# Norm factors by a power on GpSimd in place of a square root on ScalarE and a reciprocal on VectorE

## The reference

```python
def _rms_norm(x, gain):
    xf = x.astype(jnp.float32)
    y = xf * lax.rsqrt(jnp.mean(xf * xf, axis=-1, keepdims=True) + EPS)
    return (y * gain.astype(jnp.float32)).astype(x.dtype)
...
    for l in range(DEPTH):                       # first block
        xn = _rms_norm(x, attn_norm[l])
        h = xn @ w_in[l]                         # split into nine parts
        c_q = _rms_norm(h_cq, mla_q_norm[l])     # and c_kv; q and k of 16 heads are normed too
...
        o_b = (_rms_norm(o_b, diff_out_gain[l]) * (1.0 - lambda_init)).astype(x.dtype)
...
        x = x + mix @ w_o[l]
        xn = _rms_norm(x, ffn_norm[l])
        gate, up = jnp.split(xn @ w_gate_up[l], 2, axis=-1)
        x = x + (jax.nn.silu(gate) * up) @ w_down[l]
...
        x = x + rmsnorm(merged @ w_out[l], norm_mix_post[l])     # second block
        h = rmsnorm(x, norm_mem_pre[l])
        mem_n = rmsnorm(mem, norm_memkv[l])
        x = x + rmsnorm(memory_cross_attention(h, mem_n, w_mq[l], w_mkv[l], w_mo[l]), norm_mem_post[l])
        h = rmsnorm(x, norm_ffn_pre[l])
```

## Time and profile before

| | us |
|---|---|
| median of three runs | 1974.97 (1973.1 to 1977.52) |
| the profiled execution, its own time | 1970.69 |
| span of its trace | 1968.9 |
| TensorE busy in it | 1823.7 |
| VectorE busy | 1125.8 |
| ScalarE busy | 907.2 |
| GpSimd busy | 226.9 |

### The profile page before, as it was taken

One profiled execution on the slowest core, in us unless ns is written; L12 is line 12 of the kernel. 1 busy time (PEld: TensorE's weight loads), 2 busy tenths in 40 slices (PEclk: granted clock), 3 DMA queues, 4 the chain that ended last, 5 costly groups with the idle time before them and its releaser, 6 DMA issues.

```text
span 1968.9 us, 35037 instructions
## 1 busy us (share of the span) xinstructions
PE 1823.7 (93%) x13640; PEld 1709.3 (87%) x13640; DVE 1125.8 (57%) x1564; ACT 907.2 (46%) x1297; POOL 226.9 (12%) x104
## 2 busy tenths in 40 slices
PE   5999899998998899999999996999799999869997
PEld 5976799998965799998999885999789998859997
DVE  3553465542564365536564775775365647757763
ACT  5444544435354453434354455545243544555442
POOL 3520100004520200000000301000100003010000
PEclk9996999998987999999999998999899999989999
DMA  6420255444320345535534531655254445316551
GB/s 239 133 67 11 70 169 183 158 166 163 116 65 11 102 161 191 184 141 175 178 129 144 175 131 62 207 185 190 93 175 167 139 135 177 134 65 203 185 192 49
DMA packets 52447, 276.60 MB, mean 140 GB/s; under 512 B 5936, under 2 KB 6320, under 8 KB 51888
## 3 DMA queue, kind: packets, MB, share of 16 engines
q1 hardware_dynamic: 51984, 272.14, 41.2%
q10 hardware_dynamic: 288, 2.10, 0.3%
HBM read 273.16 MB, written 1.05 MB: 139 GB/s over the span
## 4 chain that ended last, share of the span: by engine, by line
PE 86%; DVE 7%; issue 4%; ACT 3%; DMA 0%; DVEq 0%; POOL 0%; ACTq 0%; SPq 0%; POOLq 0%
PE bank L704 22%; PE bank L706 21%; PE bank L707 21%; PE scores L883 2%; PE bank L663 2%; PE bank L666 1%; PE heads L908 1%; PE turned L896 1%; PE scores L716 1%; PE scores L713 1%; PE scores L715 1%; PE turned L908 1%; PE bank L1172 1%; PE bank L823 1%; PE bank L672 1%
## 5 line engine op out<-in xcount | busy, mean ns | idle before, releaser
L704 PE MATMUL bank<-x_hi,weights_lo 128*128 128x256 f32 (+1 forms) x2512 | 720.8, 287 | 5.6 <-DVE x_lo L1862 4.7
L707 PE MATMUL bank<-x_hi,weights_hi 128*128 128x256 f32 (+1 forms) x2512 | 713.1, 284 | 0.0
L706 PE MATMUL bank<-x_lo,weights_hi 128*128 128x256 f32 (+1 forms) x2512 | 713.1, 284 | 0.0
L617 DVE TENSOR_TENSOR weights_lo<-raw,weights_hi 128x1536 fp32r<-128x1536 f32 (+2 forms) x302 | 516.7, 1735 | 288.2 <-ACT weights_hi L606 287.7
L606 ACT ACTIVATE weights_hi<-raw 128x1536 fp32r<-128x1536 f32 (+3 forms) x352 | 498.2, 1439 | 118.3 <-PE bank L707 79.9
L704 PEld LDWEIGHTS bank<-x_hi,weights_lo 128*128 128x128 f32 (+1 forms) x2512 | 481.5, 192 | 13.0 <-issue 6.3
L706 PEld LDWEIGHTS bank<-x_lo,weights_hi 128*128 128x128 f32 (+1 forms) x2512 | 481.6, 192 | 2.5 <-issue 1.9
L707 PEld LDWEIGHTS bank<-x_hi,weights_hi 128*128 128x128 f32 (+1 forms) x2512 | 481.6, 192 | 0.0
L630 POOL TENSOR_TENSOR weights_lo<-raw,weights_hi 128x1536 fp32r<-128x1536 f32 (+4 forms) x50 | 165.0, 3308 | 676.1 <-ACT weights_hi L606 676.0
L706 PE MATMUL bank<-hidden_lo,weights_hi 128*128 128x256 f32 x704 | 199.6, 284 | 0.0
L707 PE MATMUL bank<-hidden_hi,weights_hi 128*128 128x256 f32 x704 | 199.6, 284 | 0.0
(11 more groups left out here) (294 smaller groups left out, 2641.1 us busy)
## 6 DMA issues: line engine op xcount, KB each, us to landing
raw<-in_w_b SPq DMA_DIRECT2D x194, 768.0 KB, 4.5
raw<-in_w_a SPq DMA_DIRECT2D x122, 768.0 KB, 4.5
raw<-in_w_a SPq DMA_DIRECT2D x14, 512.0 KB, 3.5
raw<-in_w_b SPq DMA_DIRECT2D x10, 512.0 KB, 3.9
mem<-in_mem ACTq DMA_DIRECT2D x2, 1024.0 KB, 4.9
raw<-in_w_a SPq DMA_DIRECT2D x2, 752.0 KB, 4.2
raw<-in_w_b SPq DMA_DIRECT2D x2, 752.0 KB, 4.3
raw<-in_w_b SPq DMA_DIRECT2D x2, 720.0 KB, 5.3
```

Of the source, the lines that this page charges most:

```text
L617: nc.vector.tensor_tensor(wlo[c % SPLIT][:, 0:n], raw[c % RAW][:, 0:n], whi[c % SPLIT][:, 0:n].bitcast(F32), ALU.subtract).then_inc(*s.mar ...
L704: ins = nc.tensor.matmul(dst, wl, xh, start=start, stop=False, skip_group_check=skip)
L706: nc.tensor.matmul(dst, wh, xl, start=False, stop=False, skip_group_check=skip)
L707: ins = nc.tensor.matmul(dst, wh, xh, start=False, stop=stop, skip_group_check=skip)
```

## The change

The columns of ones in the sum matmuls become columns of 1/n, so that the sum is the mean already. VectorE adds epsilon while it reads the bank (`tensor_scalar`, into `norm_mean`, `head_mean` or `dif_mean`). GpSimd raises that to the power -0.5 with a `tensor_tensor` whose second operand is a constant tile of -0.5. ScalarE takes no roots; its dummy roots are gone. What waits for a factor is as before.

```diff
-    put("half_sums", (half[:, None] == np.arange(2)[None, :]).astype(np.float32))
+    put("half_means", (half[:, None] == np.arange(2)[None, :]).astype(np.float32) / np.float32(DIF_D))
+    put("minus_half", np.full((P, 16), -0.5, np.float32))
+    for n in (DM, MLA_QR, MLA_KVR, DIF_V, MLA_QK):
+        put(f"mean_{n}", np.full((P, 2), 1.0, np.float32) / np.float32(n))
...
-        def load_root_table(tag):
-
-            n = 52 + ("o", "mem", "mo", "down", "latent").index(tag)
-            nc.scalar.activation(ROW[:, n:n + 1], eps_col, ACT.Sqrt)
-
         def scalar_norm(pl, act, l, tag, src, ready):
             scalar_squares(pl, act, l, tag, src, ready)
-            scalar_root(pl, act, l, tag)
+            if tag == "n1":
+                split_hi(pl, act, l, 1)
...
-        def scalar_root(pl, act, l, tag):
-            s = pl.s
-            if tag == "n1":
-                split_hi(pl, act, l, 0)
-            act.wait_ge(*s.at(l, "filled", f"{tag}_sum"))
-            nc.scalar.activation(NROOT[:, 0:4], pl.bank(f"{tag}_sum")[:, 0:4], ACT.Sqrt, scale=1.0 / DM, bias=eps_col)\
-              .then_inc(*s.mark("norm_root", tag))
-            if tag == "n1":
-                split_hi(pl, act, l, 1)
...
         def vector_norm_sum(pl, dve, l, tag):
             s = pl.s
-            dve.wait_ge(*s.at(l, "norm_root", tag))
-            nc.vector.reciprocal(NFACT[:, 0:4], NROOT[:, 0:4]).then_inc(*s.mark("norm_factor", tag))
+            dve.wait_ge(*s.at(l, "filled", f"{tag}_sum"))
+            nc.vector.tensor_scalar(NMEAN[:, 0:4], pl.bank(f"{tag}_sum")[:, 0:4], EPS, None, ALU.add).then_inc(*s.mark("norm_mean", tag))
...
-                ins = nc.tensor.matmul(ps[:, 2 * m:2 * m + 2], squares_of(tag)[:, 0, m * P:(m + 1) * P], ones[:, 0:2], start=True, stop=True)
+                ins = nc.tensor.matmul(ps[:, 2 * m:2 * m + 2], squares_of(tag)[:, 0, m * P:(m + 1) * P], const(f"mean_{DM}"), start=True, stop=True)
...
-                    dve.wait_ge(*s.at(l, "qk_root", name))
-                    nc.vector.reciprocal(HFACT[:, i, :], HROOT[:, i, :]).then_inc(*s.mark("qk_factor", name))
+                    dve.wait_ge(*s.at(l, "filled", f"{name}_sum"))
+                    nc.vector.tensor_scalar(HMEAN[:, i, :], pl.bank(f"{name}_sum")[:, 0:8], EPS, None, ALU.add)\
+                      .then_inc(*s.mark("qk_mean", name))
...
                     y = Y[:, 2 * i:2 * i + 2, :]
+                    dve.wait_ge(*s.at(l, "y_scaled", f"{POST[tag]}{i}"))
                     nc.vector.tensor_tensor(y, y, factor, ALU.mult).then_inc(*s.mark("norm_n", (tag, i)))
...
+        def inverse_root(pool, pl, l, out, mean, done, key):
+            s = pl.s
+            pool.wait_ge(*s.at(l, *mean[1]))
+            n = out.shape[-1]
+            nc.gpsimd.tensor_tensor(out, mean[0], const("minus_half")[:, 0:n], ALU.pow).then_inc(*s.mark(done, key))
+
         def pool_layer(pl, pool, l, order):
             pl.s.writing = "pool"
             pl.pool_next = 0
             for kind, name in order:
                 if kind == "squares" or kind == "norm" and ("squares", name) not in order:
                     pool_norm(pl, pool, l, name)
+                if kind == "norm":
+                    inverse_root(pool, pl, l, NFACT[:, 0:4], (NMEAN[:, 0:4], ("norm_mean", name)), "norm_factor", name)
+                elif kind == "latent":
+                    inverse_root(pool, pl, l, NFACT[:, 0:8], (NMEAN[:, 0:8], ("norm_mean", "latent")), "norm_factor", "latent")
+                elif kind == "turn" and pl.number == 0:
+                    i = qk_place(name)[0]
+                    inverse_root(pool, pl, l, HFACT[:, i, :], (HMEAN[:, i, :], ("qk_mean", name)), "qk_factor", name)
+                elif kind == "dif_sum":
+                    inverse_root(pool, pl, l, OFACT[:, :], (OMEAN[:, :], ("dif_mean", 0)), "dif_factor", 0)
                 elif kind == "job":
                     pool_lo(pl, pool, l, pl.last_chunk(name) + 2)
...
         @block.gpsimd
         def _(pool):
+            pool.wait_ge(loaded["const"], 16)
```

More of the change, by code:

```diff
@@ L461, in const @@
             return CM[:, a:b]
[L463 removed]
+        ident, ones, half_means = const("ident"), const("ones"), const("half_means")
         KB = (const_at["turn_dil"][0], consts.shape[1])
@@ L1030, in transformer @@
             order_a += [("map", i)] + between.get(i, [])
-        order_a += [("root_table", "o")] + [("job", f"o{i}") for i in range(4)]
+        order_a += [("job", f"o{i}") for i in range(4)]
         order_a += [("norm", "n2"), ("spread", "n2")]
@@ L1034, in transformer @@
             order_a += [("job", f"gate{i}"), ("job", f"up{i}")]
-        order_a += [("root_table", "down")] + [("job", f"down{i}") for i in range(4)]
+        order_a += [("job", f"down{i}") for i in range(4)]
         def free_a(name):
@@ L1076, in transformer @@
             elif kind == "dif_sum":
-                uses_a.append(("dif_sum", ("dif_root", 0)))
+                uses_a.append(("dif_sum", ("dif_mean", 0)))
             elif kind == "dif_spread":
@@ L1162, in tensor_a @@
                     _, at, fam, rows = next(q for q in qk_jobs if q[0] == name)
-                    heads_of = ones[0:rows, 0:2] if fam == "mla" else half_sums
+                    heads_of = const(f"mean_{MLA_QK}")[0:rows, :] if fam == "mla" else half_means
                     pe.wait_ge(*s.at(l, "qk_sq", name))
@@ L1299, in scalar_a @@
                         nc.scalar.activation(HH[:, 2 * i:2 * i + 2, :], hid(i), ACT.Copy).then_inc(*s.mark("hidden_hi", i))
-                elif kind == "latent":
-                    load_root_table("latent")
-                    act.wait_ge(*s.at(l, "filled", "latent_sum"))
-                    nc.scalar.activation(NROOT[:, 0:4], pl.bank("latent_sum")[:, 0:4], ACT.Sqrt, scale=1.0 / MLA_QR, bias=eps_col)
-                    nc.scalar.activation(NROOT[:, 4:8], pl.bank("latent_sum")[:, 4:8], ACT.Sqrt, scale=1.0 / MLA_KVR, bias=eps_col)\
-                      .then_inc(*s.mark("norm_root", "latent"))
-                elif kind == "turn":
-                    i, at, fam, rows = qk_place(name)
-                    act.wait_ge(*s.at(l, "filled", f"{name}_sum"))
-                    nc.scalar.activation(HROOT[:, i, :], pl.bank(f"{name}_sum")[:, 0:8], ACT.Sqrt,
-                                         scale=1.0 / (MLA_QK if fam == "mla" else 64), bias=eps_col).then_inc(*s.mark("qk_root", name))
                 elif kind == "spread_keys" and name == "g1":
@@ L1318, in scalar_a @@
                     scalar_map(pl, act, l, heads_a, name, out_a_hi)
-                elif kind == "dif_sum":
-                    act.wait_ge(*s.at(l, "filled", "dif_sum"))
-                    nc.scalar.activation(OROOT[:, :], pl.bank("dif_sum")[:, 0:16], ACT.Sqrt, scale=1.0 / DIF_V, bias=eps_col)\
-                      .then_inc(*s.mark("dif_root"))
                 elif kind == "dif_out":
@@ L1401, in vector_a @@
                 elif kind == "latent":
-                    dve.wait_ge(*s.at(l, "norm_root", "latent"))
-                    nc.vector.reciprocal(NFACT[:, 0:8], NROOT[:, 0:8]).then_inc(*s.mark("norm_factor", "latent"))
+                    dve.wait_ge(*s.at(l, "filled", "latent_sum"))
+                    nc.vector.tensor_scalar(NMEAN[:, 0:8], pl.bank("latent_sum")[:, 0:8], EPS, None, ALU.add)\
+                      .then_inc(*s.mark("norm_mean", "latent"))
                 elif kind == "turn":
@@ L1435, in vector_a @@
                 elif kind == "dif_sum":
-                    dve.wait_ge(*s.at(l, "dif_root"))
-                    nc.vector.reciprocal(OFACT[:, :], OROOT[:, :]).then_inc(*s.mark("dif_factor"))
+                    dve.wait_ge(*s.at(l, "filled", "dif_sum"))
+                    nc.vector.tensor_scalar(OMEAN[:, :], pl.bank("dif_sum")[:, 0:16], EPS, None, ALU.add).then_inc(*s.mark("dif_mean"))
                 elif kind == "dif_spread":
@@ L1483, in transformer @@
                     ("job", "mq0"), ("job", "mq1")] + [("map", i) for i in range(-1, MEM_H + 2)]
-        order_b += [("root_table", "mo")] + [("job", f"mo{i}") for i in range(4)] + [("norm", "p2"), ("spread", "p2"), ("norm", "n3"), ("spread", "n3")]
+        order_b += [("job", f"mo{i}") for i in range(4)] + [("norm", "p2"), ("spread", "p2"), ("norm", "n3"), ("spread", "n3")]
         for i in range(KF2 // 2):
             order_b += [("job", f"ua{i}"), ("job", f"ub{i}")]
-        order_b += [("root_table", "down")] + [("job", f"down{i}") for i in range(4)] + [("norm", "p3"), ("spread", "p3")]
+        order_b += [("job", f"down{i}") for i in range(4)] + [("norm", "p3"), ("spread", "p3")]
         QK_B = [j for i in range(3) for j in (f"q{i}", f"k{i}")]
@@ L1719, in scalar_b @@
                         scalar_norm(pl, act, l, name, X, lambda k: ("x_new", ("p3", k // 2)))
-                    elif name == "mem":
-                        scalar_root(pl, act, l, name)
-                    elif name == "n2":
```

(5 more changed lines are left out.)

24 lines of the change are left out of this document (11 added, 13 removed).

## The result

| | before | after |
|---|---|---|
| median, us | 1974.03 (4 runs, 1971.84 to 1977.52) | 2020.18 (4 runs, 2012.89 to 2023.38) |
| the profiled execution, its own time | 1970.69 | 2018.41 |
| its span | 1968.9 | 2016.6 |
| mean granted TensorE clock | 0.953 | 0.942 |

The changed kernel is slower: 1.0224 times the time before, 95% interval 1.0203 to 1.0245, or 46 us. That is the side that I had called likeliest, but 36 us above the forecast time and 9 above the end of the range.

What follows compares the result with a forecast made beforehand. TensorE, busy 93% of the span, was taken to bound the kernel. The terms 6.8 + 1.7 - 2.7 + 2.2 + 2.0 - 0.6 = +9.4 us gave 1984.4 us as the median; range 1967 to 2011.

Steps and rivals of the forecast that it cites:

- part 4: `turn` and `latent`: factors covered, GpSimd's late chunks cost nothing; only the last turn costs, +2.2 us in two layers.
- part 3: The four `n1`: held VectorE instructions released, first chunk behind the power and 0.09 us late each; together -2.7 us.
- 30t - 12.5: Whole forecast change in us as a function of t, zero at t = 0.42 us.
- t: Time of one 128x4 power on GpSimd, taken as 0.73 us; called the weakest number.
- a dear power: Rival: t above 1.6 us, more than 35 us slower, over 2010 us; chance 0.15.
- parts 1 and 2: Norms other than `n1`: 12 plain ones +6.8 us together, second block's `n2`, twice, +1.7 us.
- 0.40 + t: New TensorE idle time ahead of each plain norm's spread matmul, against 0.56 us before; 1.13 us forecast.
- part 5: `dif_sum`: the power precedes GpSimd's chunk, so L922 ends 1.0 us later; +2.0 us in two layers.
- The last `turn`: Turn uk2 at the attention's start: its late power makes L1429 start 1.1 us later; +2.2 us in two layers.
- part 6: ScalarE's table loads: only one per second-block layer, before the memory's exponentials, is on the path; -0.6 us.
- the sum of 15 us: Alternative total if GpSimd's first call of newly loaded code paid 5.95 us, as the Trainium skill says.
- growing slow-clock stretches: Sign against the prediction: slow-clock stretches behind the norms growing or shrinking by more than the steps; no size given.

Runs made afterwards that it cites:

- the mean ahead: Changed kernel, but in each first-block turn VectorE forms the mean before its two rotation products: 1988.96 us, 1.0074 times the kernel before.
- doubled powers: Changed kernel with the mean ahead, plus a second 128x4 power before the used one in each of the 18 norms: 2011.63 us, 1.0187 times the kernel before.
- first subtraction later: Kernel before, but in the four n1 norms GpSimd's first weight subtraction waits until VectorE has added up the squares: 1969.57 us, 0.9988.
- both cures: Changed kernel with each turn's mean formed before VectorE's two products and every power replaced by a multiplication of constants: 1971.34 us, 0.9994 times the kernel before.

## Why the prediction was wrong

**The step that failed is part 4**, "*`turn` and `latent`.* Their factors are used two steps later, behind whole jobs, which is the cover". That is true of the factors, and it looked at the factors alone. A `turn` gives TensorE two things back: the factor, and the bank that the sum stood in. With three banks in a ring, the product after next needs that bank. I had read that it "is now free when VectorE has read it" and costed nothing, without asking what stands ahead of that read on VectorE: a product with two SBUF inputs beside GpSimd's subtractions. The rows ahead of the prediction hold the very mechanism, at `n1`, where I used it. Held back so, the bank cost 30 of the 46 us. In the two profiled executions that is 18 us of idle time of TensorE and 13 of longer busy time at a lower clock; a sum of waits, as mine was, has no term for the second.

The same part says of GpSimd's subtractions "I cost that at nothing". They are not late for TensorE: its waits for them, 4.7 us in four, are all at `n1`, where it had waited 1.02 us each for the rounded `X` before, so that they add 0.6 us in all (part 3 had 0.4). But being pushed back by the previous power is what makes them hold the cosine product: in the turn stages, 10 us of late bank become 26.

**The power was mis-sized** in every shape: 1.02, 2.07 (1.63 where nothing disturbed it) and 2.90 us for 0.73, 1.28 and 2.4. By the prediction's own sum, 30t - 12.5, t = 1.02 gives +18 us, or 1993. The kernel with the mean ahead, which has everything of the change but the late bank, measured 1988.96. So the rest of the sum comes out in its total, and even with the right powers it would have stayed inside the range. In part that is luck. The sum counts waits alone, and with the mean ahead TensorE's idle time is only 10.7 us above the kernel before; 5.5 us more are busy time at a lower clock, for which the sum had nothing. The kernel's loss lay outside every rival I named; "a dear power" reached that time by another way.

The other parts, by the trace of the changed kernel:

- *Plain norms* (parts 1 and 2): I wrote 0.40 + t of idle time, 1.42 us at the measured t; the first norm shows 1.35, and `n2` of the second block, where VectorE is late as well, 2.20. With 1.02 in them these parts and the `n1` together give 16 times 0.86 and 2 times 1.15 us, 16 in all; the waits grew from 13.2 to 26.2 us, by 13.
- *`n1`* (part 3) went as written: the addition takes 0.43 us and the two subtractions follow the power.

```profile
17.33 0.43 DVE L798 TENSOR_TENSOR squares<-squares 128x256 f32<-128x256 f32 x1 [2.04 <-POOL squares L776]
...
18.86 0.16 DVE L786 TENSOR_SCALAR norm_mean<-bank 128x4 f32<-128x4 f32 x1 [1.10 <-PE bank L806]
...
19.11 1.02 POOL L2069 TENSOR_TENSOR norm_factor<-norm_mean,const 128x4 f32<-128x4 f32 x1 [1.88 <-DVE norm_mean L786]
20.10 4.69 POOL L633 TENSOR_TENSOR weights_lo<-raw,weights_hi 128x1024 fp32r<-128x1024 f32 x2
```

The copy in the second layer's `n1`, 1.48 us before, is 0.18 now.

```profile
467.84 0.18 DVE L1316 COPY layer_gains_a<-gains_a 128x34 f32 x1 [2.43 <-issue]
```

- *`dif_sum`* (part 5): mechanism and place as forecast, the power 0.5 us dearer. The maximum's product (L922 before) is held until the subtraction behind the power ends.

```profile
190.34 2.90 POOL L2069 TENSOR_TENSOR dif_factor<-dif_mean,const 128x16 f32<-128x16 f32 x1 [40.29 <-DVE dif_mean L1414]
193.21 3.42 POOL L633 TENSOR_TENSOR weights_lo<-raw,weights_hi 128x1536 fp32r<-128x1536 f32 x1
...
193.95 2.69 DVE L914 TENSOR_TENSOR row<-row,head_factor 128x2 f32<-128x2 f32 x1
```

- *The last `turn`*: TensorE waits 0.81 us for its factor at 150.20; forecast 1.1 a layer.
- *Table loads* (part 6): the exponential over the memory starts 0.04 us behind the maximum, as written (maximum 1219.66 to 1220.35, exponential at 1220.39). 44 us of ScalarE's time, loads and roots, are gone, and what they bought was these few tenths.
- *First call on GpSimd*: the first power lasts 1.02 us like the others. The Trainium skill's 5.95 us for newly loaded code (GPSIMD Engine Reference, section 2.1) don't appear, so the sum of 15 us that added them fell too. Whether a power runs newly loaded code at all, no run here shows.
- *The clock*: I named growing slow-clock stretches as a danger without a price. TensorE's busy time is 18.9 us longer for the same matmuls, 40% of what the span lost. The profiled execution of before was not an outlier: 23 of that kernel's 54 runs have its clock, 0.953, and the mean of them is 0.951. In two pairs of kernels the clock falls with added waits. The changed kernel and the one with the mean ahead differ by the place of one read (clock 0.938 to 0.943, against 0.945 to 0.950), and the one with doubled powers differs from the latter by its added waits (0.938 to 0.940). But fewer waits than in the kernel before didn't raise it: with the first subtraction later it is 0.946 to 0.950, lower too. What decides it the runs don't show; that stays open.

## What to carry to other kernels

When a read of a PSUM bank moves to another engine, cost the release of the bank, not only the arrival of the value: find who starts the next use of that bank, and what stands ahead of the new reader in its queue. Put such a read first. And a small instruction that is added to one engine's queue moves the large ones behind it; ask what these will then run beside, since in these traces that decided how long an instruction of VectorE or GpSimd took, where VectorE's had both operands in SBUF.

## What the runs showed of the hardware

- An elementwise power on GpSimd costs by its columns: 1.02 us for 128x4, 1.63 (undisturbed) for 128x8, 2.90 for 128x16, some 0.16 us a column and 0.4 before the first. A multiplication takes 0.20 us for 128x4 and for 128x8 and 0.21 for 128x16; only in the turns, beside VectorE's products, a 128x8 takes 0.63.
- The hold goes both ways. A power of 128x8 takes 2.07 us when VectorE's last product of the `turn` starts just before it, and 1635 ns in the median with the mean ahead; the multiplication there takes 0.63 us instead of 0.20. With the turn stages' weights on VectorE, the power of 128x16 starts 0.06 us behind a subtraction of 1.76 us on VectorE and takes 4.54 us instead of 2.90.
- Less waiting did not become less time in full. The kernel before with its first subtraction later and the one with both cures have 7.7 and 7.8 us less idle time in the profiled executions, and 8.0 and 8.1 us more busy time, at a mean granted clock of 0.948 and 0.949 instead of 0.953; both spans are 1969.2 us, against 1968.9. Over all runs the first one is 2.4 us faster, and 7 to 8 us faster where the two kernels' clocks are equal (0.948, 0.949 or 0.950). So two kernels this close are compared by their waits and their clocks, not by one time alone.
